# Swapped rotary columns in two attention mixers, and a new order of steps in a third

## The reference, cut to what matters

```python
def apply_rope(x, cos, sin):
    x1, x2 = jnp.split(x, 2, axis=-1)
    return jnp.concatenate([x1 * c - x2 * s, x1 * s + x2 * c], axis=-1)

q = rms_norm(c_q, q_norm_g) @ w_uq             # 192 -> 4 x 96
k = concatenate([k_nope, broadcast(k_rope)])   # 4 x (64 + 32)
q, k = rms_norm(q, qk_g[0]), rms_norm(k, qk_g[1])
q = concatenate([q[..., :64], apply_rope(q[..., 64:], cos, sin)])   # the same for k
softmax_causal(q k^T * 96 ** -0.5) v
```

## Time and profile before

| | us |
|---|---|
| median of three runs (1781.55 to 1785.17) | 1781.92 |
| the profiled execution | 1781.33 |
| its span, first to last instruction | 1779.5 |
| PE busy | 1765.4 |
| DVE busy | 1185.6 |
| ACT busy | 815.3 |
| mean granted clock of PE | 0.999 |

### The profile page before, as it was taken

The page is one execution under the profiler, slowest core; times in us unless marked ns, Lnnn a source line. Parts: engine busy times, 40 slices in busy tenths (PEclk is TensorE's granted clock), DMA queues, the critical chain, the costliest instruction groups (busy, mean ns, idle before and its releaser), DMA issues.

```text
span 1779.5 us, 32766 instructions
## 1 busy us (share of the span) xinstructions
PE 1765.4 (99%) x13365; PEld 1677.2 (94%) x13365; DVE 1185.6 (67%) x1869; ACT 815.3 (46%) x1087; POOL 29.2 (2%) x16
## 2 busy tenths in 40 slices
PE   9999999999999999999999999999999999999999
PEld 7879999978899999999989888999999999789999
DVE  6867986567698856675468524767567663667763
ACT  5556554346465544333346433333443332454442
POOL 0000000000000000000050000000000000000000
PEclk9999999999999999999999999999999999999999
DMA  6132556423145554455333422555444553235553
GB/s 252 72 142 97 192 188 224 165 109 143 72 166 189 212 199 166 177 195 190 131 117 132 166 84 99 185 179 198 175 164 167 185 188 122 93 141 189 189 210 121
DMA packets 35866, 284.06 MB, mean 160 GB/s; under 512 B 4800, under 2 KB 6976, under 8 KB 8256
## 3 DMA queue, kind: packets, MB, share of 16 engines
q1 hardware_dynamic: 35776, 282.78, 43.8%
HBM read 281.72 MB, written 1.05 MB: 159 GB/s over the span
## 4 chain that ended last, share of the span: by engine, by line
PE 91%; DVE 6%; ACT 2%; issue 1%; DMA 0%; DVEq 0%; ACTq 0%
PE PS L1362 24%; PE PS L1367 24%; PE PS L1363 24%; PE PS L873 3%; PE PS L706 3%; PE PS L1264 2%; PE PS L729 2%; PE PS L752 1%; PE PS L1153 1%; PE PS L1024 0%; DVE QK L2186 0%; PE PS L838 0%; DMA wa<-in_wmix 0%; DVE W L2476 0%; PE PS L845 0%
## 5 line engine op out<-in xcount | busy, mean ns | idle before, releaser
L1362 PE MATMUL PS<-Hhi,split 128*128 128x272 f32 (+1 forms) x2176 | 537.6, 285 | 1.4 <-DVE Hlo L2139 1.2
L1363 PE MATMUL PS<-Hlo,split 128*128 128x256 f32 (+1 forms) x2080 | 509.8, 283 | 0.0
L2111 DVE TENSOR_TENSOR split<-wa,split 128x2048 fp32r<-128x2048 f32 (+2 forms) x174 | 358.7, 2062 | 123.2 <-ACT split L1506 123.2
L1362 PEld LDWEIGHTS PS<-Hhi,split 128*128 128x128 f32 x2176 | 408.8, 188 | 2.7 <-DVE Hlo L2139 1.9
L1363 PEld LDWEIGHTS PS<-Hlo,split 128*128 128x128 f32 x2080 | 391.6, 188 | 0.2
L1506 ACT CAST split<-wa 128x2048 fp32r<-128x2048 f32 (+2 forms) x174 | 299.4, 1721 | 63.7 <-PE PS L1367 60.9
L1367 PE MATMUL PS<-Hhi,split 128*128 128x256 f32 (+1 forms) x2080 | 274.8, 285 | 0.0
L1362 PE MATMUL PS<-hidhi,split 128*128 128x256 f32 (+1 forms) x1088 | 268.1, 285 | 0.5 <-DVE hidlo L2768 0.5
L1363 PE MATMUL PS<-hidlo,split 128*128 128x256 f32 (+1 forms) x1088 | 267.4, 284 | 0.0
L1367 PEld LDWEIGHTS PS<-Hhi,split 128*128 128x128 f32 x2080 | 261.9, 188 | 0.0
L1362 PEld LDWEIGHTS PS<-hidhi,split 128*128 128x128 f32 x1088 | 205.0, 188 | 1.0 <-DVE hidlo L2768 0.9
(11 more groups left out here) (402 smaller groups left out, 2383.6 us busy)
## 6 DMA issues: line engine op xcount, KB each, us to landing
wa<-in_wfi SPq DMA_DIRECT2D x126, 1024.0 KB, 4.8
wa<-in_wfo SPq DMA_DIRECT2D x48, 1408.0 KB, 6.0
wa<-in_wmix SPq DMA_DIRECT2D x25, 2048.0 KB, 7.9
wa<-in_wmix SPq DMA_DIRECT2D x4, 1536.0 KB, 7.0
H<-in_wfi SPq DMA_DIRECT2D x3, 1024.0 KB, 10.7
G<-in_wfi SPq DMA_DIRECT2D x3, 1024.0 KB, 4.9
wa<-in_wmix SPq DMA_DIRECT2D x2, 1024.0 KB, 4.8
wa<-in_wmix SPq DMA_DIRECT2D x1, 1824.0 KB, 7.4
```

The costliest lines, as they stand in the source:

```text
L1362: pe.matmul(o, hi, xhi, start=first, stop=False)
L1363: pe.matmul(o, hi, xlo, start=False, stop=False)
L2111: dve.tensor_tensor(out=wlo[n % 2][:, at:width], in0=wa[:, c % 2, at:width], in1=whi[n % 2][:, at:width].bitcast(F32), op=ALU.subtract).th ...
```

## The change

Two things are changed.

In the first two mixers the query weights get 32 more columns per head: the rotary columns with their two halves swapped. So a query tile has 128 rows, 64 plain, 32 rotary, 32 swapped. The mean square still takes rows 0 to 95. The table `rope[:, 2, :]` holds cosines in rows 0 to 95 (of the angle 0 in rows 0 to 63) and signed sines in rows 96 to 127, and one multiplication turns the queries; the sum of the two terms is left to the score product, whose contraction has 128 rows. The keys get their swapped columns out of a wider `krsel`; VectorE turns them and adds both terms in rows 64 to 95, and ScalarE copies these rows to rows 96 to 127 for the score product. The rotation products and the constant `rot_mla` go. `wm` grows from 1408 to 1664 columns. The split column 6 no longer waits for the MLA queries and keys, only for the roots.

In the last mixer the value product moves ahead of the keys' mean square, the third column group behind the second scores, the banks of the column groups are exchanged, the pooled product goes between the two head groups' values, each output tile takes k 4 to 7 (pooled rows) before k 0 to 3, and the steps on ScalarE's and VectorE's lists are moved with them. The early load into H waits for the last column group in place of the value product.

```diff
-WM = 2 * 384 + 4 * 96 + 256
+WM = 2 * 512 + 4 * 96 + 256
...
+c[96 + (j + 16) % 32, CC["krsel"] + 96 + j] = 1.0
...
-of_mla = NormSignals(S.ml_raw, S.ml_sq, S.ml_ms, S.ml_rs, S.ml_n, S.ml_rot, S.ml_done)
+of_mla = NormSignals(S.ml_raw, S.ml_sq, S.ml_ms, S.ml_rs, None, None, S.ml_done)
...
-    return norm_plan((lane_ml, lane_mk)[k], SEQ, 4, 0, lane_ml.QK[0:96, 4 * k:4 * k + 4, 0:SEQ],
-                     gains=[A(f"mlak{l}" if k else f"mlaq{l}", 0, 96)] * 4, rows=96, width=96, rot=rope_mla, sig=of_mla)
+    return norm_plan((lane_ml, lane_mk)[k], SEQ, 4, 0, lane_ml.QK[:, 4 * k:4 * k + 4, 0:SEQ],
+                     gains=[A(f"mlak{l}" if k else f"mlaq{l}")] * 4, width=96, rot=rope_mla, sig=of_mla, tall=(96,) * 4)
...
-    sp.wait_ge(S.odd_v, 1)
+    sp.wait_ge(S.dx_tile, 4)
     load_early(5, 0)
     sp.wait_ge(S.pool_out, 1)
     load_early(5, 1)
...
         for h in range(4):
-            o = places[SEQ][0:96, 4 + h, :]
-            pe.matmul(o, wm[:, 96 * h:96 * h + 96], CQ[:, 0, 0:SEQ], start=True, stop=False)
-            mm = pe.matmul(o, wm[0:HD, 384 + 96 * h:480 + 96 * h], CQ[0:HD, 1, 0:SEQ], start=False, stop=True)
+            o = places[SEQ][:, 4 + h, :]
+            pe.matmul(o, wm[:, P * h:P * h + P], CQ[:, 0, 0:SEQ], start=True, stop=False)
+            mm = pe.matmul(o, wm[0:HD, 512 + P * h:512 + P * h + P], CQ[0:HD, 1, 0:SEQ], start=False, stop=True)
         mm.then_inc(S.q_up, 1)
         pe.wait_ge(S.kr_ready, upto(S.kr_ready))
         for h in range(4):
-            o = places[SEQ][0:96, 8 + h, :]
-            pe.matmul(o, wm[:, 768 + 96 * h:864 + 96 * h], CKV[:, 0:SEQ], start=True, stop=False)
-            mm = pe.matmul(o, C("krsel", 96), KR[:, 0:SEQ], start=False, stop=True)
+            o = places[SEQ][:, 8 + h, :]
+            pe.matmul(o, C("krsel", P), KR[:, 0:SEQ], start=True, stop=True)
+            mm = pe.matmul(o[0:96, :], wm[:, 1024 + 96 * h:1120 + 96 * h], CKV[:, 0:SEQ], start=False, stop=True,
+                           skip_group_check=True)
         mm.then_inc(S.k_up, 1)
         mean_square(q_mla)
         tokens_half(0, 0)
-        tokens(wm[:, 1152:1408].unsqueeze(1), 0, 256, TILES1, [(7, 0), (7, 256)], src=CKV.unsqueeze(1),
+        tokens(wm[:, 1408:1664].unsqueeze(1), 0, 256, TILES1, [(7, 0), (7, 256)], src=CKV.unsqueeze(1),
                kt=1).then_inc(S.mv_in, 1)
         mean_square(k_mla)
         tokens_half(0, 1).then_inc(S.v_in, 1)
-        rotate(q_mla)
         pe.wait_ge(S.qk_ready, upto(S.qk_ready))
         stick_scores(1)
         pe.wait_ge(S.mv_out, upto(S.mv_out))
         tokens_half(1, 0)
-        rotate(k_mla)
         tokens_half(1, 1).then_inc(S.mx_used, 4)
         take(4)
...
+        pe.wait_ge(S.ml_rs, upto(S.ml_rs, 0))
+        split_column(6, 8)
         pe.wait_ge(S.ml_done, upto(S.ml_done, 2))
-        split_column(6, 8)
         soft_scores(mla, 0)
...
         def stream(i):
+            if i == 1:
+                pe.wait_ge(S.v_ready, upto(S.v_ready))
             if i >= 2:
                 pe.wait_ge(S.dx_out, i - 1)
-            mm = tiles(wd, [(P * (3 - i), P, 6 + i % 2)], TT)
+            mm = tiles(wd, [(P * (3 - i), P, 7 - i % 2)], TT)
             mm.then_inc(S.dx_tile, 1)
-        def window_project(m, ks, first, last):
+        def window_project(m, ks):
...
-                pe.matmul(o, hi[:, k, :], Ohi[:, k, :], start=first and m % 2 == 0 and k == ks[0], stop=False,
+                pe.matmul(o, hi[:, k, :], Ohi[:, k, :], start=m % 2 == 0 and k == KD // 2, stop=False,
                           skip_group_check=True)
                 pe.matmul(o, lo[:, k, :], Ohi[:, k, :], start=False, stop=False, skip_group_check=True)
             if m == 0:
-                pe.wait_ge(S.od_lo, 2 if ks[0] == 0 else 6)
+                pe.wait_ge(S.od_lo, 6 if ks[0] == 0 else 5)
             for k in ks:
-                mm = pe.matmul(o, hi[:, k, :], Olo[:, k, :], start=False, stop=last and k == ks[-1],
+                mm = pe.matmul(o, hi[:, k, :], Olo[:, k, :], start=False, stop=k == KD // 2 - 1,
                                skip_group_check=True)
-            if last:
+            if ks[0] == 0:
                 mm.then_inc(S.od_used, 1)
...
         mean_square(q)
+        tokens(w, 256, P, KEYS3, [(6, 0), (6, P), (6, 2 * P)]).then_inc(S.odd_v, 1)
         mean_square(k)
         wd = use(2, base, KD, 512)
         stream(0)
...
             attend_scores(swa[g], 1)
         stream(1)
         attend_transposes(swa[0], 1)
-        stream(2)
         attend_transposes(swa[1], 1)
         for g in range(2):
             pe.wait_ge(S.sm_ptc, upto(S.sm_ptc))
             attend_scores(swa[g], 2)
+        stream(2)
         stream(3)
-        pe.wait_ge(S.dx_out, 3)
-        tokens(w, 256, P, KEYS3, [(6, 0), (6, P), (6, 2 * P)]).then_inc(S.odd_v, 1)
         for g in range(2):
             attend_transposes(swa[g], 2)
-        pe.wait_ge(S.v_ready, upto(S.v_ready))
-        for g in range(2):
-            pe.wait_ge(S.sm_ptc, upto(S.sm_ptc))
-            attend_values(swa[g])
+        pe.wait_ge(S.sm_ptc, upto(S.sm_ptc))
+        attend_values(swa[0])
         take(2)
         pe.wait_ge(S.pm_in, 16)
         pe.wait_ge(S.pool_y, upto(S.pool_y))
         for g in range(4):
             mm = pe.matmul(pool_place(g), wm[:, P * g:P * g + P], POOLED[:, g, META:TT], start=True, stop=True)
         mm.then_inc(S.pool_out, 1)
-        pe.wait_ge(S.od_hi, 2)
-        for m in range(PER_ODD):
-            window_project(m, range(4), True, False)
-        pe.wait_ge(S.od_hi, 6)
+        pe.wait_ge(S.sm_ptc, upto(S.sm_ptc))
+        attend_values(swa[1])
         for m in range(KD):
-            window_project(m, range(4, KD) if m < PER_ODD else range(KD), m >= PER_ODD, True)
+            for ks, ready in ((range(KD // 2, KD), 5), (range(KD // 2), 6)):
+                if m == 0:
+                    pe.wait_ge(S.od_hi, ready)
+                window_project(m, ks)
         xs[0] += KD
...
         stick_log(1)
+        act.wait_ge(S.ml_turn, upto(S.ml_turn))
+        act.copy(k_mla.dst[96:P, :, :], k_mla.dst[HD:96, :, :]).then_inc(S.ml_done, 1)
         for n in range(8, 10):
             round_piece(n)
         soft_exp(mla, 0)
...
-            act.copy(DX[:, 3 - i, :], PS[:, 6 + i % 2, 0:TT]).then_inc(S.dx_out, 1)
+            act.copy(DX[:, 3 - i, :], PS[:, 7 - i % 2, 0:TT]).then_inc(S.dx_out, 1)
...
         for g in range(2):
             attend_exp(swa[g], 1)
         stream(1)
-        attend_copies(swa[0], 1)
-        stream(2)
-        attend_copies(swa[1], 1)
+        for g in range(2):
+            attend_copies(swa[g], 1)
+        round_piece(0)
+        round_piece(1)
         attend_exp(swa[0], 2)
         attend_exp(swa[1], 2)
+        stream(2)
         stream(3)
         for g in range(2):
             attend_copies(swa[g], 2)
-        round_piece(0)
-        round_piece(1)
-        round_window(0)
         round_piece(2)
         round_piece(3)
-        round_window(1)
+        round_window(0)
         act.wait_ge(S.pool_out, 1)
         for g in range(4):
             act.activation(Ohi[:, 4 + g, :], pool_place(g), ACT.Copy, scale=A("dscale", g)).then_inc(S.od_hi, 1)
+        round_window(1)
         round_piece(4)
         round_piece(5)
         round_early(0)
+        act.wait_ge(S.od_used, 2)
+        round_early(1)
         round_piece(6)
         round_piece(7)
-        round_early(1)
         project_out(SEQ, META, "ffn2g1", KD // PER_ODD, True)
...
+    def turned_queries(q):
+        chain(normalised(q))
+        dve.tensor_tensor(out=q.dst, in0=q.lane.W[2][:, 0:4, 0:SEQ], in1=per_head(q.rot, 4),
+                          op=ALU.mult).then_inc(q.sig.done, 1)
+    def turned_keys(k):
+        w0, w2 = (k.lane.W[i][:, 0:4, 0:SEQ] for i in (0, 2))
+        own, other, both = slice(HD, 96), slice(96, P), slice(0, 96)
+        chain(normalised(k))
+        dve.tensor_tensor(out=k.dst[both, :, :], in0=w2[both, :, :], in1=per_head(k.rot[both, :], 4), op=ALU.mult)
+        chain(dve.tensor_tensor(out=w0[own, :, :], in0=w2[other, :, :], in1=per_head(k.rot[other, :], 4),
+                                op=ALU.mult))
+        dve.tensor_tensor(out=k.dst[own, :, :], in0=k.dst[own, :, :], in1=w0[own, :, :],
+                          op=ALU.add).then_inc(S.ml_turn, 1)
...
-        turned(q_mla)
+        turned_queries(q_mla)
         dve.wait_ge(S.mv_in, upto(S.mv_in))
         for kt in range(2):
             ins = copy_heads(lane_ml.VP, P, kt, 0, 4, PS[:, 7, 256 * kt:256 * kt + 256])
         ins.then_inc(S.mv_out, 1)
         rest_piece(6)
-        turned(k_mla)
-        turned_sum(q_mla)
+        turned_keys(k_mla)
         stick_scaled(1)
         dve.wait_ge(S.v_in, upto(S.v_in))
         copy_heads(VP, P, 0, 0, 8, PS[:, 6, :]).then_inc(S.v_out, 1)
-        turned_sum(k_mla)
         rest_piece(7)
         stick_softplus(1)
         product(base + 2)
...
-            dve.wait_ge(S.od_hi, g + 1)
```

(17 more changed lines are left out.)

33 lines of the change are left out of this document (16 added, 17 removed).

## The result

The changed kernel took 1771.92 us, median of six runs (1771.13 to 1776.92), the kernel before 1781.85 us beside it (1781.55 to 1785.17): a ratio of 0.9949, 95% interval 0.9937 to 0.9960. The prediction was 1772.1 us, in a range of 1768.6 to 1777.5. The profiled execution took 1771.87 us with a span of 1770.1; before it was 1781.33 and 1779.5. The gain to explain is 9.4 us of span.

A forecast was written before the change was run, and what follows sets the result against it. TensorE, busy for 1765.4 of 1779.5 us, was taken as the bound. Gains of 5.0 (two first mixers), 3.0 (last mixer) and 1.2 us (behind the projection) sum to 9.2, from 1781.33 to 1772.1 us; range 1768.6 to 1777.5.

The forecast's parts named there:

- The mixers: First two mixers: rotation products leave TensorE, VectorE loses the keys' late pair; 2.5 us a layer, 5.0 us for both.
- VectorE's lag binds: First two mixers: TensorE could come 3.4 us earlier per layer, but waits 0.8 us for VectorE's operands before the second scores.
- Rival (a): First two mixers: VectorE's lag does not bind, TensorE's whole 6.8 us come; 1770.3 us, chance 0.17.
- Weight loads: First two mixers: 16 query weight loads widen from 96 to 128 columns, costing 0 to 0.5 us, taken as 0.2.
- The hold on VectorE: First two mixers: the keys' second product, reading another quadrant with no wait before it, costs 0 to 0.1 us more, taken as 0.1.
- The last mixer to the feed-forward block: Last mixer reordered: 0.4, 0.4, 2.2 us of waits and 1.7 us of slow clock go, 0.9 and 0.8 come; 3.0 us gained.
- The two new waits: Last mixer: TensorE waits 0.9 us between the groups' first transposes and 0.8 us before the second group's transposes next round.
- Behind the projection: Head of the next feed-forward block: VectorE's 2.3 us lag on tiles 6 and 7 goes, and the 1.2 us Hlo wait.
- Rival (b): Last mixer: the clock falls in the new waits, 1.7 us each; 1773.8 or 1775.5 us, chance 0.17.
- Rival (d): Last mixer: clock falls at the first new wait and stays low through the projection; 1784.9 us and up, chance 0.02.
- (c): First two mixers: ScalarE's copy lands on the path, later casts pile up, a layer keeps nothing; 1777.1 us, chance 0.06.
- (e): Last mixer: a chunk or cast is late, the 2.2 us wait stays with its clock loss; 1776.0 us, chance 0.05.

## Why the prediction was right, point by point

**The mixers: 5.0 predicted, 4.7 measured.** The step that mattered was "VectorE's lag binds": of 3.4 us that TensorE alone would give, 2.4 came. TensorE itself came 3.27 us earlier in place of 3.4, measured at the first score block; the keys' rotation, which I had priced like the queries' at 1.82 us, took 1.54 in the trace of the kernel before (388.30 to 389.84). The wait before the second scores was 0.4 us rather than 0.8, because 0.2 of it is taken earlier, at L848; that the lag is 0.8 in all, with 0.2 that the list of waits doesn't show, comes from the run without the keys' two steps. Up to the second score block the second mixer gained 2.47 us, just the 2.5 of the forecast; the 2.3 in the table is over the whole way to the last mixer, which varies between runs: 1154.82 in the kernel before and 1154.54 with the same code in the run of the last mixer's part alone, and 1151.60 to 1153.19 in eight traces with the change's code there, six of them within 0.3 us. Whole runs give a little less than the 4.7: at a mean clock of 1.000, seven runs of the last mixer's part alone have a median of 1775.84 us, ten of the change 1771.9, so the mixers' part is worth 3.9 us there. Part of the difference may be the start, which was 0.2 us later in the changed kernel's trace; what else is in it is open. Rival (a), the whole 6.8 us, is out with it: with TensorE setting the pace the mixers would be 1.6 us shorter still.

**Weight loads: 0.2 predicted, 0.2 measured.** From the second on, the eight query groups of a layer start 0.63 us apart in place of 0.60, and all eight take 4.91 us in place of 4.73. The kernel before, and then the changed one:

```profile
35.56 0.67 PE L903 MATMUL PS<-G,wm 128*96 128x256 f32 x2
36.16 0.67 PE L904 MATMUL PS<-G,wm 64*96 64x256 f32 x2
```

```profile
35.82 0.70 PE L899 MATMUL PS<-G,wm 128*128 128x256 f32 x2
36.45 0.70 PE L900 MATMUL PS<-G,wm 64*128 64x256 f32 x2
```

**The hold on VectorE: 0.1 predicted, 0.1 measured.** The keys' second product (L2211) starts at 383.62 and the sum, which waits for it, at 384.87, 1.25 us later; from the first product (L2210) to the second, with no wait between, it is 1.24 us, not the 1.14 of the unwaited pair in the earlier trace rows. The Trainium skill (VectorE: DVE Perf Modes, "Two Vector instructions with no wait between them") holds such an instruction, whose input begins in another quadrant, until the earlier one is finished; this trace agrees.

**The ScalarE copy: nothing predicted, nothing measured**, with a cover of 0.4 us where I had 0.3.

**The last mixer to the feed-forward block: 3.0 predicted, 2.9 measured.** The two new waits were forecast as 0.9 and 0.8 us and are 0.88 and 0.68. The reason of the second holds too: VectorE came to its maximum straight from the pooled tiles. The 0.4 + 0.4 + 2.2 us that were to go went. The slow clock was put at 1.7 us, and the projection is 1.5 us shorter. There is a second reading of that term, from whole runs. Of the 50 runs of the kernel before in the three groups, 11 had a mean clock of 1.000, and their median is 1779.74 us. Against the change's 1771.92 that is 7.8 us, so 1.6 less than the 9.4 of the two traces. A mean clock below 1.000 is thus a thing of most runs of the kernel before (39 of 50), and of one in eleven of the change's. That it is in each of them the fall behind this wait is likely but not shown, since only one execution of the kernel before has a trace.

**Behind the projection: 1.2 predicted, 2.0 measured.** This is the term that was mis-sized. The mechanism was as stated: VectorE is no longer late with the sums of tiles 6 and 7. But I took its price from the list of waits alone. TensorE's timeline of the kernel before shows three late starts behind the projection, of which the list has only the middle one:

```profile
1589.65 0.28 PE L1363 MATMUL PS<-Hlo,split 128*128 128x256 f32 x1
1589.88 0.39 PE L1362 MATMUL PS<-Hhi,split 128*128 128x256 f32 x1
...
1590.34 0.28 PE L1363 MATMUL PS<-Hlo,split 128*128 128x256 f32 x1
1591.86 0.39 PE L1362 MATMUL PS<-Hhi,split 128*128 128x256 f32 x1 [1.24 <-DVE Hlo L2139]
...
1592.33 0.28 PE L1363 MATMUL PS<-Hlo,split 128*128 128x256 f32 x1
1592.72 0.38 PE L1362 MATMUL PS<-Hhi,split 128*128 128x256 f32 x1
```

Starts lie 0.12 us apart in the dense run. The three gaps of 0.23, 1.52 and 0.39 us hold 0.1 + 1.4 + 0.3 = 1.8 us more than that. The product behind each late one starts 0.22 to 0.23 us after it, another 0.1 us each, which makes 2.1 us; in the changed kernel none of these gaps is left, and the block behind got 2.0 us shorter. Starts have to be compared, for a matmul's recorded duration covers part of each gap. The run with the last mixer's part alone has the same 190.03 us, the one with the mixers alone 192.19, so the gain comes from the new order of the last mixer. Which of its moves brings it, the earlier rest of the early weights or the steps before it, no run shows.

The two small misses, 0.8 more here and 0.3 + 0.1 less in the mixers and the last one, with 0.2 of a later start, brought the sum 9.2 to 9.4. That 1772.1 came out to 0.2 us is in part luck: these misses cancel, and the start and the way from the second mixer to the last vary by more than that between runs.

**Rival (b), the clock falls in the new waits,** is not what the change's profile shows: 1.00 over both waits. By the rule that I set beside it (the Trainium skill, TensorE: Matmul & The Clock Gate, "Part 4: PE-mode transpose": a transpose doesn't count as busy in the same way) it would have been the likeliest. The stretch of 3.2 us from 1531.35, 2.1 us of it transposes and 1.1 us idle, brought no fall, so here the trace doesn't bear the rule out. One of the change's eleven runs did have a mean clock of 0.998 and took 1776.92 us, 1.4 us above the 1775.5 that this rival gave for two falls; it has no trace, so where its clock was low is open. The direction of the fear was sound, though. With 4.1 us of idle ahead of the same transposes the mean clock was 0.998 or lower in all ten runs. **Rival (d), it stays low and the kernel is slower,** had 0.02 and needed 25 us at half clock; the run without the column group had some 18 us in half of its executions, behind a longer wait than the change has. **Rivals (c) and (e)** are out by the runs on the copy and on the rows.

## What to carry to other kernels

When work is taken off the engine that is always busy, look for the engine that prepares its operands: here 3.4 us off TensorE were worth 2.4 us, since VectorE's list ahead of the next operand got no shorter than that. A wait filled with work from elsewhere comes back at the next meeting point when the other engine sets the pace, as the quarter of a column group showed. And price a stall from the spacing of starts, not from the list of waits.

## What the runs showed of the hardware that I had not expected

The fall of the clock doesn't sit at a fixed distance from the idle time. It came 0.8 us into the idle of the run without the column group, about 2.5 us after idle began in the kernel before (1560.9 to 1563.4), and 4.1 us after in the run with the mixers alone (1556.2 to 1560.3), there with 1.7 us of dense products at full clock in between. In each of the three the low level then lasted from 3.4 to about 7 us.

In these traces a fall cost only what ran on TensorE during it. The one in the kernel before lay over 3.5 us of dense products and cost 1.5 us (24.35 against 22.83 in the projection); the one without the column group lay half over idle time and over transposes that had a wait of 0.9 us to fill.

The time of one kernel goes with its mean granted clock, run by run. The kernel before took 1779.3 to 1781.1 us at 1.000 (11 runs), 1780.3 to 1782.1 at 0.999 (25), 1781.6 to 1784.4 at 0.998 (9) and 1783.8 to 1787.2 below (5); neighbouring groups overlap. A median of few runs partly says how often the clock fell in them.
